# Decode attention: four instead of two of a sequence's eight value pages get their low parts on GpSimd

## What is computed

```python
k_past = cache_k[page_table].reshape((db, past_len) + cache_k.shape[2:])
v_past = cache_v[page_table].reshape((db, past_len) + cache_v.shape[2:])
s = jnp.einsum('bqhcd,bkhcd->bhcqk', q, kp) * ATTN_SCALE      # 8 heads, 2 parts c
p = jax.nn.softmax(jnp.concatenate(scores, axis=-1), axis=-1)
w = p[:, :, 0] - lam * p[:, :, 1]
out = out + jnp.einsum('bhqk,bkhe->bqhe', w[..., start:start + s_len], vp)
```

## Time and profile before

| | us |
|---|---|
| median of 3 runs | 1901.7 (1901.42 to 1903.68) |
| profiled execution, its own time | 1898.74 |
| its span | 1896.6 |
| TensorE matmuls busy | 1703.2 (90%) |
| VectorE busy | 1042.4 (55%) |
| ScalarE busy | 839.5 (44%) |
| GpSimd busy | 320.4 (17%) |
| mean granted TensorE clock | 0.941 |

### The profile page before, as it was taken

One profiled execution on the slowest core, in us unless ns is written; L12 is line 12 of the kernel. 1 busy time (PEld: TensorE's weight loads), 2 busy tenths in 40 slices (PEclk: granted clock), 3 DMA queues, 4 the chain that ended last, 5 costly groups with the idle time before them and its releaser, 6 DMA issues. The chain is left out here.

```text
span 1896.6 us, 31172 instructions
## 1 busy us (share of the span) xinstructions
PE 1703.2 (90%) x9243; PEld 1384.7 (73%) x9243; DVE 1042.4 (55%) x2696; ACT 839.5 (44%) x1994; POOL 320.4 (17%) x814
## 2 busy tenths in 40 slices
PE   4299999999999997997999999999999588887798
PEld 3287887878788785777878778778788466665476
DVE  4534445444443444344777767767766466676443
ACT  5244434333343332243555545555545366665322
POOL 1011212212121120010122221221222012111101
PEclk8699999999999997998999999999999789898799
DMA  5123050340413103132211211211100567767713
GB/s 154 36 56 72 22 92 2 90 81 11 92 14 78 27 11 135 52 129 63 61 56 40 65 50 42 58 54 44 39 23 26 200 228 259 272 227 237 263 58 110
DMA packets 164757, 171.97 MB, mean 91 GB/s; under 512 B 14634, under 2 KB 133834, under 8 KB 164658
## 3 DMA queue, kind: packets, MB, share of 16 engines
q1 hardware_dynamic: 161538, 170.78, 30.6%
q10 hardware_dynamic: 3120, 0.01, 0.1%
HBM read 141.85 MB, written 28.91 MB: 90 GB/s over the span
## 5 line engine op out<-in xcount | busy, mean ns | idle before, releaser
L1016 PE MATMUL PS<-WH,XH 128*128 128x512 f32 x512 | 212.5, 415 | 0.0
L1016 PE MATMUL PS<-WH,XL 128*128 128x512 f32 x512 | 201.9, 394 | 0.0
L1016 PE MATMUL PS<-WL,XH 128*128 128x512 f32 x512 | 201.9, 394 | 0.0
L1997 PE MATMUL PS<-W,XH 128*128 128x512 f32 x384 | 123.8, 403 | 0.0
L2423 PE MATMUL PS<-cst,RAW 128*128 128x128 f32 x512 | 87.3, 322 | 40.5 <-DVE XL L2330 34.9
L1751 ACT ACTIVATE WORK<-PD,WORK 128x896 f32<-128x896 f32 (+7 forms) x128 | 94.9, 741 | 62.7 <-DVE WORK L1918 57.6
L1016 PEld LDWEIGHTS PS<-WH,XL 128*128 128x128 f32 x512 | 96.2, 188 | 22.8
L2423 PEld LDWEIGHTS PS<-cst,RAW 128*128 128x128 f32 x512 | 68.5, 165 | 58.7 <-DVE XL L2330 42.6
L1016 PEld LDWEIGHTS PS<-WH,XH 128*128 128x128 f32 x512 | 96.7, 189 | 19.8
L1016 PEld LDWEIGHTS PS<-WL,XH 128*128 128x128 f32 x512 | 96.8, 189 | 17.1
L2330 DVE TENSOR_TENSOR XL<-PS,XH 128x512 fp32r<-128x512 f32 x128 | 83.9, 684 | 38.2 <-ACT XH L2251 38.1
(11 more groups left out here) (361 smaller groups left out, 4575.4 us busy)
## 6 DMA issues: line engine op xcount, KB each, us to landing
RAW<-in_cache_k SPq DMA_DIRECT2D x64, 512.0 KB, 4.7
WORK<-in_cache_v SPq DMA_DIRECT2D x64, 512.0 KB, 4.6
RAW<-in_w_in_a SPq DMA_DIRECT2D x40, 512.0 KB, 7.0
out<-WORK SPq DMA_DIRECT2D x16, 512.0 KB, 3.0
out<-RAW SPq DMA_DIRECT2D x16, 512.0 KB, 3.2
RAW<-in_w_in_b SPq DMA_DIRECT2D x60, 128.0 KB, 2.3
RAW<-in_w_kv SPq DMA_DIRECT2D x56, 128.0 KB, 2.3
WORK<-d_G SPq DMA_DIRECT2D x8, 528.0 KB, 12.1
```

What stands on the lines that cost most here:

```text
L1016: last = nc.tensor.matmul(bank, x[:, k, tok(t, P)], wkvoz(w)[:, k, :], start=(k == i == 0), stop=(k == KT - 1 and i == 2))
L1997: last = nc.tensor.matmul(out, x[:, k, at(NT - 1 - s)], w[:, k, cols], start=(k == i == 0), stop=(k == KT - 1 and i == 2))
```

## The change

GpSimd's loop covers pages 1, 3, 5 and 7 of a sequence, VectorE's program pages 0, 2, 4 and 6. So odd pages are counted on `vlp` and even pages on `vl`, four of each per sequence, and the waits of SyncE (before a load) and of TensorE (before a value page) count accordingly. Orders, slots, loads and matmuls are the same.

```diff
@@ -2177,12 +2177,8 @@
 
                     def values(i, p, following=True):
 
-                        if p % 4 == 3:
-                            wait(sp, vlp, 2 * i + p // 4)
-                        elif p >= 4:
-                            sp.wait_ge(vl, 6 * i + (p - 3))
-                        elif following:
-                            sp.wait_ge(vl, 6 * i - (2 - p))
+                        if p >= 4 or following:
+                            sp.wait_ge(vlp if p % 2 else vl, 4 * i + (p // 2 - 1))
                         src = cache_v[page(sp, i * PAGES + p), :, :, :]
                         sp.dma_start(VB[:, p % 4, :], src.rearrange("a p h e -> (a p) (h e)"))\
                           .then_inc(v_ld[p % 4], 16)
@@ -2226,7 +2222,7 @@
                 @block.gpsimd
                 def _(pool):
                     with pool.Fori(0, DB) as i:
-                        for p in (3, 7):
+                        for p in (1, 3, 5, 7):
                             pool.wait_ge(vh, PAGES * i + p + 1)
                             nc.gpsimd.tensor_tensor(VL[p % 4], VB[:, p % 4, :], VH[p % 4].bitcast(F32), ALU.subtract)\
                               .then_inc(vlp, 1)
@@ -2396,7 +2392,7 @@
                                 shares()
                             elif step == "W" and values:
                                 weights_low()
-                            elif step[0] == "V" and values and int(step[1]) % 4 < 3:
+                            elif step[0] == "V" and values and int(step[1]) % 2 == 0:
                                 v_low(int(step[1]))
                     sequences(dve, body, links, 4)
 
@@ -2450,10 +2446,7 @@
 
                         def value(p):
 
-                            if p % 4 == 3:
-                                pe.wait_ge(vlp, 2 * i + p // 4 + 1)
-                            else:
-                                pe.wait_ge(vl, 6 * i + (p + 1 if p < 3 else p))
+                            pe.wait_ge(vlp if p % 2 else vl, 4 * i + p // 2 + 1)
                             if p == 0:
                                 pe.wait_ge(wlo, i + 1)
                                 wait(pe, avc, i)
```

## The result

The changed kernel took 1912.7 us in the median of 5 runs (1911.2 to 1914.2), the kernel before 1903.3 us (5 runs, 1901.4 to 1903.7). The ratio is 1.0052 with a 95% interval of 1.0037 to 1.0067. A second set of 6 runs gave 1915.2 against 1903.0 us and a ratio of 1.0063 (1.0050 to 1.0076). The forecast was 1914.6 us, 12.9 us over the median of before that was on record then (1901.7 us).

What follows compares the result with a forecast made beforehand. No single engine was taken as the bound: they take turns, and the last score matmuls wait for VectorE's last key page. 7 x 1.68 + 1.15 = 12.9 us over the 1901.7 us median gave 1914.6 us, range 1908 to 1921.

Steps and rivals of the forecast that it cites:

- The two moved passes never stood in a queue: Decode stage, VectorE: low parts of pages 1 and 5 start 0.04 and 0.03 us after their high parts end.
- A pass on GpSimd takes 2.39 us and starts 0.07 us behind the high part: Decode stage, GpSimd: each of 16 added low-part passes takes 2.39 us, starting 0.07 us after ScalarE's high-part copy.
- VectorE's pass ends 1.07 us behind the GpSimd pass that it falls into: Decode stage: a VectorE low part of values starting inside a GpSimd pass ends 1.07 us after that pass.
- First delay 0.54, second 1.14, together 1.68 us a sequence: Page 2 comes 0.54 us late in the front half; by the back half the last score matmuls are 1.68 us late.
- What delays S3 delays every later sequence: Lateness of a sequence's last score matmul group, 1.68 us, is carried in full into the next sequence.
- without slack: From the last score matmuls the next sequence follows directly, through VectorE's reduction of their rows before the first keys' low parts.
- Loads moved at no cost: SyncE issues page 5's load 1.2 us later and page 6's 0.5 to 0.7 us later, costed at nothing.
- Last sequence 1.15 us late: Eighth sequence, values only: GpSimd's page 3 comes 1.15 us late behind VectorE's page 2, delaying page 7's load and the end.
- The sum: Decode stage: seven sequences at 1.68 us plus 1.15 us in the last make 12.9 us.
- The clock does not fall: TensorE keeps its 2.4 GHz clock despite idling about 1.4 us before page 5, so no clock cost is added.
- the rival: TensorE's clock drops to 1.2 GHz after idling before page 5, adding 16 us for 1931 us; chance 9%.

Runs made afterwards that it cites:

- the runs with one page: Against the kernel before, GpSimd makes low parts of pages 1, 3, 7 in one run and 3, 5, 7 in the other: ratios 1.0023 and 1.0027.
- K7 first: Kernel before, with the last key page's high and low parts and the last score matmuls put ahead of value page 6: ratio 0.9997 (0.9985 to 1.0010).
- page 1 alone: Kernel before, but GpSimd makes low parts of pages 1, 3 and 7 while page 5 stays with VectorE: ratio 1.0023 (1.0010 to 1.0036).

## Why the prediction was right

- *The two moved passes never stood in a queue.* Right. Taking them away from VectorE made nothing earlier: in windows of 201 us the wait for VectorE's low parts of values fell by 8.8 us, and 17.0 us of waiting for GpSimd replaced it. The 18 us off VectorE's busy time did not come: it fell from 1042.4 to 1038.6 us, as a pass that stands still is recorded as busy.
- *A pass on GpSimd takes 2.39 us and starts 0.07 us behind the high part.* Right: 2.37 to 2.40 us outside the last sequence; 1600.76 + 1.04 + 0.07 = 1601.87.
- *VectorE's pass ends 1.07 us behind the GpSimd pass that it falls into.* Right: 1.08 to 1.09 us in all 16 such passes, in the sequence above in recorded passes of 1.93 and 2.14 us (1.9 and 2.6 were named; page 6's record is shorter as its own high part came 0.30 us late, and in the seven sequences it was 1.84 to 2.44 us). The run without the second SBUF operand took the long passes away. The rule of the Trainium skill ("SBUF — State Buffer", section "Who interferes with whom") agrees with these rows in who stands still and which operands decide it; a whole pass of 1.22 us behind GpSimd's end they do not show.
- *First delay 0.54, second 1.14, together 1.68 us a sequence.* Right: 0.55 and 1.12 in the changed kernel, each alone in the runs with one page.
- *What delays S3 delays every later sequence.* Right for this delay: the stretch from S3's rows to the next exponential stayed at 4.64 us. But the way named for it, VectorE's steps on S3's rows, was not the last to end. In the kernel before, VectorE then sits 0.72 us until ScalarE has copied the next queries, and ScalarE comes to those behind the finished rows, for which it waits 1.66 us for N on TensorE:

```profile
1612.32 1.07 ACT L2303 ACTIVATE WORK<-PD 64x512 f32<-64x512 f32 x2 [1.66 <-PE PD L2469]
```

```profile
1613.68 0.42 DVE L2358 TENSOR_TENSOR WH<-WORK,WH 64x32 fp32r<-64x32 f32 x2 [0.72 <-ACT WH L2271]
```

N stands behind S3 and page 7, so a later S3 reaches the next sequence this way. K7 first showed that it does not hold the other way, and in the second profile of the kernel before up to 0.75 us more in this stretch was made up for the most part ahead of the next R0. So "without slack" was too strong.

- *Loads moved at no cost.* Right in the sum by luck, wrong as a step: page 6's load did come late, and it cost nothing only since page 5's slow pass lay over it. With page 1 alone it cost 2.5 us in the back half. I had worked out a landing for page 5's load and none for page 6's.
- *Last sequence 1.15 us late.* GpSimd's page 3 was: it ends 11.90 us behind the last exponential's start, before 10.75, with VectorE ahead of it. From that exponential to the last store it took 26.6 and 26.4 us in the two profiles of the changed kernel, and 25.9 and 24.8 in those of the kernel before: 0.5 to 1.8 us, so the term is right within what repeats.
- *The sum.* 7 x 1.67 = 11.7, plus 0.7 in the last sequence and 0.7 in the stretches ahead of R0 (the eight of them, taken together), less 0.1 in what is left; the decode stage as a whole lost 13.0 us. The medians show 9.4 and 12.2 us. That the stages ahead of decode move by up to 6 us between executions of one kernel I had not seen from a single trace; it is also why the profiled execution of before was not a firm base for the total.
- *The clock does not fall.* Right where the rival had it, at the wait before page 5 and at S3. Between 1611.5 and 1615.5 us, across that wait, TensorE was busy 2.72 of 4.00 us and the granted clock stayed at the upper level, 2.4 GHz:

```profile
1611.50:1615.50 4.00, 2.72 (x11) 0.93 (x9) 3.34 (x3) 2.66 (x4) 2.51 (x2) 1.00 0.97 307
```

The column behind GpSimd's busy time is the clock, 1.00. Ahead of R0, where the first key pages of a sequence are turned, it is another matter. From the exponential to R0 the clock is at its lower level (1.2 GHz) for 6.8 us in each of the seven sequences of the kernel before. In the changed kernel it is so in five of them, and in two, the same two in both profiles, for 9.9 to 10.0 us. One of those two and one of the five:

```profile
1622.55:1638.04 15.49, 13.21 (x78) 11.63 (x79) 9.64 (x18) 8.23 (x14) 0.00 (x0) 0.68 0.64 205
1658.83:1673.38 14.55, 11.96 (x78) 10.19 (x79) 9.65 (x18) 8.13 (x14) 0.00 (x0) 0.77 0.66 215
```

The column gives the mean granted clock: 0.68 of 15.49 us makes 2 x 0.32 x 15.49 = 9.9 us at half clock, 0.77 of 14.55 us makes 6.7. The two sequences take 15.5 us here, the five 14.4 to 15.3; with page 1 alone the stretch took 14.1 to 16.3 us, and the longest had 10.2 us at the lower level. So the change did bring more time at the lower clock, 6.2 us in all in these stretches, while the stretches together lost 0.7 us. What part of that is the clock's no run tried, and why it stays low for longer in two sequences is open.

## What to carry to other kernels

Before work is moved to an idle engine, look whether the step that is moved ever stood in a queue; if it started as soon as its input was there, and the steps behind it gain little, the move adds the difference of the two engines' speeds. Moving half of a chain of subtractions from VectorE to GpSimd also set the two against each other here wherever both read two operands from SBUF, and what paid was whatever stood behind VectorE's pass, the last key page. And in a loop with two nearly level ways a delay of both was passed on, where speeding up one of them gained nothing.

## What the runs showed that was not expected

Which engine stood still went by who was ahead: in the last sequence VectorE's page 2 waited for GpSimd's page 1, and then GpSimd's page 3, ready as well, waited until VectorE had read (3.36 us recorded, 2.24 of them behind VectorE's end). A VectorE subtraction of the same size with one operand in PSUM ran through beside GpSimd in 1.22 us. Between executions of one kernel the stages ahead of the decode stage moved by up to 6 us while the decode stage itself repeated within 0.6. And the changed kernel spent more time at the lower clock in a place that no rival had named, ahead of R0.
